# Sixteen modulation units moved into the first attention, and 26 ticks of the second group dealt over the first selection

## The reference

```python
mod = silu(c) @ w_mod + b_mod                    # 6 x 1024 per stream
sh1, sc1, gt1, sh2, sc2, gt2 = split(mod, 6)
h = rmsnorm(x, norm1_gain) * (1 + sc1) + sh1
gq, gk, gv, gr, glr, dq, dk, dv, gates = split(h @ w_in)
y_a = gla(gq, gk, gv, decay(glr)) * silu(gr) @ w_gla_out      # gated linear attention, 4 heads
y_b = diff_attend(rope(norm(dq)), rope(norm(dk)), dv) @ w_diff_out   # two softmax maps a head, 8 heads
x = x + gt1 * ((sigmoid(g_a) * y_a + sigmoid(g_b) * y_b) @ w_out)
h2 = rmsnorm(x, norm2_gain) * (1 + sc2) + sh2
q = h2 @ w_pq                                    # 8 retrieval heads, two halves of 128
v1, i1 = top_k(q1 @ sub_keys1.T, 16); v2, i2 = top_k(q2 @ sub_keys2.T, 16)
sc, ci = top_k(v1[:, None] + v2[None, :], 16)    # 16 of 256 pairs: experts idx, weights g
x = x + gt2 * sum_k(g * gelu(h2 . peer_u[idx]) * peer_v[idx])
```

## Time and profile before

| | |
|---|---|
| time, median of 3 runs | 4507.81 us (4505.8 to 4512.99) |
| profiled execution | 4508.04 us, of it the span of the trace 4505.9 |
| TensorE, VectorE, ScalarE, GpSimd busy | 69, 60, 31, 27% of the span |
| bytes moved | 1531.57 MB, of them the gathers 1107.36 |
| first gather issued / first dots / last dots' products | 494.1 / 509.5 / 4491.5 us |

### The profile page before, as it was taken

How to read it: one execution, slowest core, us unless ns; L and a number is a source line. 1 busy time by engine, 2 the same in 40 slices (tenths; PEclk the granted TensorE clock), 3 DMA queues, 4 the chain that set the end, 5 groups by cost and what they waited for, 6 DMA issues and landing times.

```text
span 4505.9 us, 48754 instructions
## 1 busy us (share of the span) xinstructions
PE 3110.6 (69%) x15864; PEld 1988.0 (44%) x15864; DVE 2683.7 (60%) x7531; ACT 1402.5 (31%) x2980; POOL 1234.7 (27%) x1067
## 2 busy tenths in 40 slices
PE   5776498797878769668786688757776776433333
PEld 3666376485555337446453366534333454200000
DVE  1132634623866884536868864466679845686675
ACT  2341346602255550112555621033446401000000
POOL 0000111101223332322233322322334323344443
PEclk7778699898878789879788799878778788655555
DMA  7546565678989999999899999999999999999997
GB/s 268 187 150 240 195 244 207 229 261 308 373 320 385 360 365 381 386 367 383 323 406 360 345 391 368 391 353 365 359 381 402 405 388 404 401 399 410 400 408 329
DMA packets 285716, 1531.57 MB, mean 340 GB/s; under 512 B 48136, under 2 KB 93288, under 8 KB 112760
## 3 DMA queue, kind: packets, MB, share of 16 engines
q0 software_dynamic: 152064, 1107.36, 62.1%
q1 hardware_dynamic: 133400, 421.09, 25.5%
HBM read 1487.21 MB, written 40.01 MB: 339 GB/s over the span
## 4 chain that ended last, share of the span: by engine, by line
DMA 22%; PE 21%; DVE 13%; issue 6%; ACT 3%; SPq 2%; POOL 1%; DVEq 0%; ACTq 0%; POOLq 0%
DMA rt_ring<-in_peer_uv,rt_few_idx 13%; PE rt_acc L853 5%; DVE rt_ring L1618 5%; PE pair L610 4%; PE pair L599 3%; DMA dense<-scratch_mod 3%; DMA scratch_scores<-dense 3%; PE bank L610 2%; PE pair L766 2%; PE bank L599 2%; DVE rt_diag L1629 1%; DMA w<-in_weights 1%; DVE negmax L1465 1%; DMA scratch_vh<-dense 1%; POOL rt_ring L1671 1%
## 5 line engine op out<-in xcount | busy, mean ns | idle before, releaser
L1671 POOL DMA_INDIRECT rt_ring<-in_peer_uv,rt_few_idx x1056 | 1231.3, 1166 | 3238.2 <-PE rt_acc L853 2566.3
L1618 DVE SCALAR_TENSOR_TENSOR rt_ring<-rt_ring,rt_h 128x1024 f32<-128x1024 f32 x1056 | 1261.8, 1221 | 400.8 <-DMA rt_ring<-in_peer_uv,rt_few_idx 370.3
L853 PE MATMUL rt_acc<-rt_ring,rt_diag 128*32 128x512 f32 x4224 | 770.1, 804 | 656.8 <-DVE rt_diag L1629 655.9
L610 PE MATMUL pair<-dense,w 128*128 128x256 f32 (+2 forms) x3024 | 585.4, 352 | 23.5 <-DMA w<-in_weights 22.7
L599 PE MATMUL pair<-w,dense 128*128 128x256 f32 (+1 forms) x2304 | 556.5, 401 | 32.3 <-DMA w<-in_weights 26.9
L610 PEld LDWEIGHTS pair<-dense,w 128*128 128x128 f32 x3024 | 505.3, 195 | 138.8 <-issue 65.6
L853 PEld LDWEIGHTS rt_acc<-rt_ring,rt_diag 128*32 128x32 f32 x4224 | 100.7, 122 | 999.2 <-DVE rt_diag L1629 869.0
L1180 ACT ACTIVATE rt_act_dot<-rt_dot 128x2 f32<-128x2 f32 x528 | 106.7, 203 | 1365.5 <-DVE rt_ring L1618 1353.7
L599 PEld LDWEIGHTS pair<-w,dense 128*128 128x128 f32 (+1 forms) x2304 | 435.8, 192 | 181.1 <-issue 64.6
L1629 DVE TENSOR_SCALAR rt_diag<-cst,rt_act_dot,rt_few_prob 128x32 f32<-128x32 f32 x1056 | 266.4, 297 | 155.9 <-ACT rt_act_dot L1180 144.7
L610 PE MATMUL bank<-dense,w 128*128 128x256 f32 (+2 forms) x1456 | 287.3, 355 | 5.3 <-DMA w<-in_weights 4.1
(11 more groups left out here) (233 smaller groups left out, 3172.4 us busy)
## 6 DMA issues: line engine op xcount, KB each, us to landing
w<-in_weights SPq DMA_DIRECT2D x284, 1024.0 KB
rt_ring<-in_peer_uv,rt_few_idx POOLq DMA_INDIRECT x1056
rt_h<-scratch_h SPq DMA_DIRECT2D x132, 128.0 KB
dense<-scratch_mod SPq DMA_DIRECT2D x22, 512.0 KB, 17.9
dense<-in_x_prompt SPq DMA_DIRECT2D x16, 512.0 KB, 7.2
scratch_scores<-dense SPq DMA_DIRECT2D x64, 128.0 KB
rt_sc<-scratch_scores SPq DMA_DIRECT2D x8, 1024.0 KB
rt_x<-scratch_x SPq DMA_DIRECT2D x132, 32.0 KB
```

Of the source, the lines that this page charges most:

```text
L610: mm = nc.tensor.matmul(bank[b][:, 0:n], wt[:, k * CH + j * P:k * CH + (j + 1) * P], src[:, k, 0:n], start=(k == 0), stop=(k == KC - 1))
L853: mm = nc.tensor.matmul(acc[u % 2][a * T:(a + 1) * T, :], diag[b % 2][:, i, :], slot[:, D + c * BANK:D + (c + 1) * BANK], start=(q == 0), ...
L1618: dt = nc.vector.scalar_tensor_tensor(up, up, 1.0, h2[u % 2][:], ALU.mult, ALU.mult, accum_out=dot[:, b % 2, i:i + 1])
L1671: nc.gpsimd.indirect_dma_start(ring[n % RING][:], None, d["peer_uv"], bass.IndirectOffsetOnAxis(ap=few_idx[u % 2][:, c:c + 1], axis=0)).th ...
```

## The change

The late modulation's 16 units leave the dk and dv blocks. They stand one behind each of the 16 attention ticks of tile 0, in the order of the loads too. They sum in `rt_acc`, the banks of the routed part, which is idle then; their rows lie in the last buffers of `rt_ring`, as do bias and gain of all six parts. Tile 0's attention no longer takes k and v through the weight ring, but as two transfers at the first dq tick into a third ring buffer. The bank rotation of dk and dv of tile 0 goes over six banks, not five. In `sequence()` the first 26 ticks of group 1 (4 norm, 14 dk, 8 dv) move from the steps into the selection of tile 0: eight before its first step, 18 spread over the steps behind. The rest of group 1's ticks is dealt over the same 38 steps.

```diff
-ARENA, FILLS = 12928, 7
+EARLY, EARLY_1 = 26, 8
+ARENA, FILLS = 12928, 8
...
-    late = [("mod", part, u) for part in range(2, 6) for u in range(4)] if g == 0 else []
     for kind in ("dk", "dv"):
-        for i in range(4):
-            names += [(kind, i)] + late[:2]
-            late = late[2:]
+        names += [(kind, i) for i in range(4)]
...
-    names += [("kv", m) for m in range(len(kv_loads(g)) + kv_lag(g))]
+    if g == 0:
+        names += [("mod", part, u) for part in range(2, 6) for u in range(4)]
+    else:
+        names += [("kv", m) for m in range(len(kv_loads(g)) + kv_lag(g))]
...
-            late(i if kind == "dk" else 4 + i)
...
-    out.extend((("at", g, k), c) for k, c in enumerate(attend_costs(g)))
+    late = [("mod", 2 + u // 4, u % 4) for u in range(16)] if g == 0 else []
+    for k, c in enumerate(attend_costs(g)):
+        out.append((("at", g, k), c))
+        if late:
+            if late[0][2] == 0 and late[0][1] > 2:
+                out.append((("modrow", late[0][1] - 1), 0.5))
+            out.append((late.pop(0), 1.0))
+    assert not late
+    if g == 0:
+        out.append((("modrow", 5), 0.5))
...
-    fill = [tick for tick, _ in ticks(0)] + select(GROUPS[0][0]) + [("unit", 0), ("unit", 1)]
...
+    chain, early, pos = select(GROUPS[0][0]), EARLY, 0
+    fill = [tick for tick, _ in ticks(0)] + chain[:1]
+    for i, step in enumerate(chain[1:]):
+        upto = EARLY_1 + (early - EARLY_1) * i // (SELECT - 6)
+        fill += [tick for tick, _ in lane[pos:min(early, upto)]] + [step]
+        pos = min(early, upto)
+    fill += [("unit", 0), ("unit", 1)]
+    spent = sum(c for _, c in lane[:pos])
...
-    nxt, steps, spent, pos = 2, [], 0.0, 0
+    marks[0], nxt, steps = spent, 2, []
...
+        mbias = ring[RING - 1][:, 0:6 * CH].rearrange("p (m c) -> p m c", c=CH)
+        mrow = ring[RING - 1][:, 6 * CH:8 * CH].rearrange("p (m c) -> p m c", c=CH)
+        mgain = ring[RING - 2][:, 0:2 * CH].rearrange("p (m c) -> p m c", c=CH)
+        k_first = ring[RING - 3][:, 0:D].rearrange("p (h t) -> p h t", h=DH)
+        v_first = ring[RING - 3][:, D:2 * D].rearrange("p (h c) -> p h c", h=DH)
...
+                late = part_ > 1
+                if late:
+                    dst, n = acc[part_ % 2], part_ - 2
+                    if u == 0 and part_ > 3:
+                        pe.wait_ge(late_free, part_ - 3)
...
-                    slot = (g, "kv", kv_load_of(g, x))
-                    wt = weights(slot)
+                    if g == 0:
+                        pe.wait_ge(kv_first, 32)
+                        keys_of = k_first[:, h, :]
...
-                    elif g == 0:
-                        act.wait_ge(md_row, 6)
-                        for i in range(2):
-                            act.wait_ge(md_out[i], 128)
...
+                    if g == 0 and tick == 0:
+                        stored(0)
+                        sp.dma_start(k_first, d["kT"][:, :, 0:P].rearrange("h p t -> p h t")).then_inc(kv_first, 16)
+                        sp.dma_start(v_first, d["vh"][:, :, 0:VD].rearrange("h p c -> p h c")).then_inc(kv_first, 16)
```

More of the change, by code:

```diff
@@ L149, in add @@
         out.extend(((kind, g, i), cost) for i in range(count))
[L151 to L156, removed]
     if g == 0:
@@ L457, in trunk @@
         acc = [ctx.enter_context(nc.psum_tensor(f"rt_acc{u}", [P, BANK], F32)) for u in range(2)]
-        ALL, FIVE = list(range(6)), list(range(5))
+        ALL = list(range(6))
         const_in, filled, act_step, dve_step = sem("const_in"), sem("filled"), sem("act_step"), sem("dve_step")
@@ L554, in mod @@
                 wt = weights((0, "mod", part_, u))
-                if u == 0:
-                    b, n = take(("mod", part_), [5] if part_ > 1 else ALL)
+                late = part_ > 1
[3 more added lines that the diff above has]
+                        pe.wait_ge(late_free, part_ - 3)
+                elif u == 0:
+                    b, n = take(("mod", part_), ALL)
                     pe.wait_ge(bank_free[b], n)
                     pe.wait_ge(c_ready, 1)
-                b, n = sessions["mod", part_]
+                if not late:
+                    b, n = sessions["mod", part_]
+                    dst = bank[b]
                 for kk in range(2):
                     for q in range(4):
-                        mm = nc.tensor.matmul(bank[b][q * 32:(q + 1) * 32, 0:CH], c_pad[:, 2 * u + kk, :],
+                        mm = nc.tensor.matmul(dst[q * 32:(q + 1) * 32, 0:CH], c_pad[:, 2 * u + kk, :],
                                               wt[:, (kk * 4 + q) * CH:(kk * 4 + q + 1) * CH],
                                               start=(u == 0 and kk == 0), stop=(u == 3 and kk == 1))
-                if u == 3:
+                if u == 3 and late:
+                    mm.then_inc(late_made, 1)
+                    released[0, "mod", part_, u] = (late_made, n + 1)
+                elif u == 3:
                     mm.then_inc(bank_made[b], 1)
@@ L616, in rotary @@
                 nt = len(GROUPS[g])
-                among = FIVE if g == 0 and kind == "dk" else ALL
+                among = ALL
                 if kind == "dk" and n == 0:
@@ L641, in dv @@
                     i, ti = n // nt, n % nt
-                    released[g, "dv", i] = tokens(("dv", g, i, ti), weights((g, "dv", i)), ti, hT, FIVE if g == 0 else ALL)
+                    released[g, "dv", i] = tokens(("dv", g, i, ti), weights((g, "dv", i)), ti, hT, ALL)
             def gla_qk(kind, g, p, j):
@@ L752, in attend @@
                     n, nk = width(t), key_count(t)
-                    slot = (g, "kv", kv_load_of(g, x))
-                    wt = weights(slot)
+                    if g == 0:
+                        pe.wait_ge(kv_first, 32)
+                        keys_of = k_first[:, h, :]
+                    else:
+                        slot = (g, "kv", kv_load_of(g, x))
+                        keys_of = weights(slot)
                     wide = nk > BANK or (x > 0 and key_count(GROUPS[g][units[x - 1][1]]) > BANK)
@@ L775, in attend @@
                     n, tiles = width(t), key_tiles(t)
-                    slot = (g, "kv", kv_load_of(g, x) + kv_lag(g))
-                    v = weights(slot)[:, D:].rearrange("p (t c) -> p t c", c=VD)
+                    if g == 0:
+                        v = v_first[:, h:h + 1, :]
+                    else:
+                        slot = (g, "kv", kv_load_of(g, x) + kv_lag(g))
+                        v = weights(slot)[:, D:].rearrange("p (t c) -> p t c", c=VD)
                     pe.wait_ge(at_copied, session_of[G] + 1)
@@ L890, in finished @@
             if kind == "at":
-                return [(a[0], "kv", m) for m in kv_done[a[0]].get(a[1], ())]
+                return [(a[0], "kv", m) for m in kv_done[a[0]].get(a[1], ())] if a[0] > 0 else []
             if kind == "merge":
@@ L1227, in modrow @@
                 i = part_ % 2
-                b, before = sessions["mod", part_]
                 if part_ == 0:
@@ L1661, in _ @@
         def _(pool):
-            for dst, value in ((c_pad[:], 0.0), (arena[:, 4608:6656], 0.0), (state[:], 0.0), (rms[:], 1.0), (ams[:], 1.0),
+            for dst, value in ((c_pad[:], 0.0), (mbias, 0.0), (mgain, 0.0), (state[:], 0.0), (rms[:], 1.0), (ams[:], 1.0),
                                (eps[:], EPS), (one[:], 1.0)):
```

22 lines of the change are left out of this document (15 added, 7 removed).

## The result

The changed kernel takes **4442.9 us** (median of 4 runs, 4440.85 to 4450.89) against 4508.0 (4 runs): ratio 0.9858, 95% interval 0.9845 to 0.9871, so about 64 us (1.4%) faster. The forecast was 4424, in a range from 4405 to 4445. The profiled execution is 63.7 us shorter than the one before (span 4442.2 against 4505.9).

A forecast was written before the change was run, and what follows sets the result against it. No engine is full; up to the first selection's end one tile's work runs alone with a different limit per stretch, then TensorE limits, and DMA from 1104. Sum: 4508.0 - 47 + 8 - 45 = 4424 us, range 4405 to 4445.

The forecast's parts named there:

- Part 1: Tile 0's dk and dv without late modulation: 47 us in place of 94.3, a gain of 47, bounds 35 to 57.
- Part 2: Late modulation's units enter tile 0's attention, mostly hidden after the first seven ticks: +8 us, bounds +1 to +31.
- Rival A: Attention pays in full, each tick waiting for its load: +31 in place of +8, 4447 us; chance 0.12.
- Part 3: 26 ticks dealt over the selection: product 53 us earlier less 8 for steps, a gain of 45, bounds 15 to 58.
- The first selection step: On VectorE, 23.4 us later behind the first eight ticks; the selection's end 36 us later.
- The step that failed: Behind the selection, the next product waits through ScalarE for the first dots: 550 instead of 603.4, 53 us earlier.
- Steps pushed into the rest: Five steps formerly done before the product spread over the later gla and attention chains: 5 to 15 us, taken as 8.
- The remainder: From the last keys of group 1 to the end, both programs alike: 3402 us, within 10.
- B: Early ticks give nothing, the later first gather taking back the steps' gain: 4469 us; chance 0.13.
- C: More than forecast: dk and dv 37 us, attention +3, Part 3 at 58: 4396 us; chance 0.08.
- D: Slower: the first gather, late by 72 us through VectorE's waits, sets the end: 4541 us; chance 0.04.
- E: No change: the first gather sets the end, with the expected delay of 36 us: 4505 us; chance 0.03.

The follow-up runs named there:

- experiment 7: Changed kernel with the 16 late units placed in attention ticks 6 to 15, none in 0 to 5: 4454.1 us, ratio 0.9879.
- experiment 3: Kernel before with only the 26 ticks dealt over the selection, late modulation left in dk and dv: 4486.0 us, ratio 0.9945.
- experiment 2: Changed kernel with no ticks dealt over the selection, only the late modulation moved: 4471.5 us, ratio 0.9913.
- Experiment 4: Changed kernel with 28 early ticks instead of 26, and 4 instead of 8 ahead of the selection: 4424.5 us, ratio 0.9809.
- Experiment 1: Changed kernel with 28 instead of 26 ticks dealt over the selection, so the last value stores precede the first units: 4427.0 us, ratio 0.9819.
- the sixth: On top of experiment 5, the second group's keys due 22 instead of 26 steps ahead of its first unit: 4431.1 us, ratio 0.9832.
- experiment 5: On top of Experiment 4, 12 more second-group ticks behind the first two units' requests, ahead of the first dots: 4429.5 us, ratio 0.9818.
- experiment 8: Changed kernel with the second routed unit's 16 small requests moved from the selection's end to the sixth step: 4430.5 us, ratio 0.9831.
- experiment 9: Experiment 4 with the second routed unit's 16 small requests moved to the sixth step: 4409.2 us, ratio 0.9792.
- experiment 10: Experiment 5 with the second routed unit's 16 small requests moved to the sixth step: 4403.0 us, ratio 0.9776.

## Why the prediction was right, and where it was off

**What bounds the kernel.** Right: no work was removed, all gains are waits, and what was won by the keys' end mostly arrived (63.7 us of 70.4).

**Part 1, -47.** It gave 51.9. dk and dv took 42.4 us. The k stores again stood in the way, but for 3.9 us, not 7:

```profile
59.53 6.49 SPq L1794 DMA_DIRECT2D out_k_prompt<-dense  x2
64.71 0.43 DVE L1353 TENSOR_TENSOR dense<-dense 128x256 f32<-128x256 f32 x1 [3.86 <-DMA out_k_prompt<-dense]
```

dv then started at 69.8, 26.4 us after dk and not 29, and its four blocks ran in 15.9 us. I had taken 18, in the middle between the low-clock block of the earlier trace rows and the fast ones of the earlier trace rows; the row below has 64 products in 16.08 us, 4.0 a block:

```profile
69.84 16.08 PE L623 MATMUL pair<-w,dense 128*128 128x256 f32 x64
```

**Part 2, +8.** It was +6.5, for the reason given. From the first score to the transpose in the eighth tick it took 12.3 us before and 18.1 now (I had said 19 to 24), which is 5.9 of the 6.5; from there on ScalarE's chain hides the units. TensorE:

```profile
204.26 0.80 PE L794 MATMUL pair<-rt_ring,dense 64*128 64x128 f32 x4 [0.76 <-ACT dense L1010]
205.00 1.93 PE L583 MATMUL rt_acc<-w,c_pad 128*32 128x256 f32 x16
...
212.05 1.07 PE L583 MATMUL rt_acc<-w,c_pad 128*32 128x256 f32 x16
...
221.38 1.07 PE L583 MATMUL rt_acc<-w,c_pad 128*32 128x256 f32 x16 [1.31 <-DMA w<-in_weights]
222.39 0.33 PE L769 MATMUL bank<-cst,dense 128*128 128x128 f32 x1
...
231.52 1.93 PE L583 MATMUL rt_acc<-w,c_pad 128*32 128x256 f32 x16
```

Rival A fails: the units' products waited for their loads 2.8 us in all, their weight loads into TensorE 4.0. The mean granted clock of the stretch went from 0.50 to 0.79 with TensorE busy 34.7 of 47.8 us where it had been 17.5 of 41.3, and inside it nine units took 1.07 us each, six 1.93 or 1.94, and one 1.25. The Trainium skill (TensorE: Matmul & The Clock Gate, section on the HAM clock gate) states the direction, that activity lifts the throttled clock; the trace agrees, with 0.79 against 0.50. The measured +6.5 lies halfway between the +5 that I had named for a level that rises and my +8. It didn't rise for good: the three units from 231.52 to 239.09 take 1.93 or 1.94 again, the first of them behind gaps of 2.4 and 0.5 us. The price of a wrong place is known from experiment 7: +20 in place of +6.5.

**Part 3, -45: this term was mis-sized; it gave 23** (70.4 at the keys' end, less the 47.2 by which the last keys of tile 0 came earlier, at 375.9 instead of 423.1). Alone, in experiment 3, it gives 19.4 by trace and 16 to 33 by time; on top of experiment 2 it is 27.3 by trace. Step by step:

- The first selection step was to come 23.4 us later relative to the keys of tile 0: 22.4. The selection's end 36: 33.4. Both right. Experiment 4 shows 6 us of this to be VectorE's wait at the head.
- The step that failed: "The next product needs ScalarE, which waits for the first dots: 550." With the parts 1 and 2 as measured, that is 503, and 522.0 is 19 us behind it. ScalarE didn't wait for the first dots, which began at 496.1, but until 519.0 for the last store of values, and the product came at 522.0. I had counted the ticks up to the 26th and taken the place behind them for free, though two dv ticks were left out of the dealing. They hold no product, only one eviction on ScalarE (at 466.16, 0.38 us) and the last four stores on SyncE. For tile 0 I had written that ScalarE waits at gq for the last v store; for the second group I didn't ask where that store now stands in SyncE's list. Experiment 1 puts them in front: 500.9, within 2 us of the forecast.
- Steps pushed into the rest, +8: 11.1 (500.6 to 511.7 us from the product to the keys' end). TensorE has 32 more products there, four steps of eight, and is busy 13.4 us longer. I had counted five steps; the fifth's products, at 604.47, stand inside the stretch in both kernels. Four steps at 1.06 us are 4.2; the rest goes with the lower granted clock, 0.88 against 0.91, in the two rows shown above (busy time multiplied by clock is 396 and 397). What lowers the clock there is open.

**The remainder.** The claim was that from 1104 on both programs take the same 3402 us, within 10. It is 3408.5, 6.6 more, so the claim held within its margin. I suspected the banks, whose rotation the change shifts; experiment 3 keeps it and has 3413.7. Over the traces of this study (but the sixth's, whose keys are due later) the same stretch takes 3396.5 to 3420.2 us: 3401.1, 3409.0, 3413.7, 3420.2 and 3403.3 in experiments 1 to 5, then 3403.5, 3397.8, 3398.5 and 3396.5 in experiments 7 to 10. No part of the change goes with the long ones: the two longest, 3413.7 and 3420.2, come from executions that were 14.5 and 14.6 us above the median of their kernels. The three shortest are those of experiments 8 to 10, which share the second unit's later requests and also the chip; which of the two it is, or chance, is open. With runs of one kernel up to 32 us apart (experiment 3), a difference of 7 is no effect that these traces can show.

**The rivals.** B, that the early ticks give nothing, falls by experiment 3. C is half right in its first term (dk and dv at 42.4, halfway from 47 to its 37), and in no other. D and E needed the delayed gather to set the end; it was delayed by 33 us as feared, and the stretch shrank by more. The forecast stood 19 us too low by the median, 20 by the profiled execution (4444.0): parts 1 and 2 were 8 better than said (47 against 39), part 3 22 worse, the remainder 7 worse. That the time stayed in the range, by 2 us, is in part luck: without the 8 us more of parts 1 and 2 the same error in part 3 would have put it near 4451.

## What to carry to other kernels

When work is moved ahead of a burst of transfers, move it to its last store: a tick that only stores is cheap in every engine's busy time and can still hold a buffer, and behind the burst it cost 21 us here. When the first wait behind a stage is removed, look at once at who is next in SyncE's list; here the order of its requests came with 10 and 28 us at the keys' end (experiments 9 and 10), ScalarE's order without it with a loss of 8 (experiment 5). And a plan that cuts a list by count should cut it where a buffer is released.

## What the runs showed of the hardware

- A store of 128 KB landed 4.9 us after its issue in front of ten gathers of 1 MB (experiment 1), and 22.6 and 24.8 us after it behind them (changed kernel, experiment 8), with the view's DMA share at 1.03 and 1.02; in experiment 1 it was 0.76 meanwhile.
- Sixteen small requests of one unit hold SyncE for 9 to 10 us (476.4 to 486.1 in the changed kernel's trace), with four groups of four that start 2.8, 2.6, 2.4 and 2.0 us apart, the 4 KB ones first and no shorter than those of 128 and 32 KB. I hadn't counted that as a price for what is queued behind.
- A late unit takes 1.93 us at 205.0, at the head of the attention, and 1.07 at 212.05, with TensorE without a gap in between; at 231.52, behind a gap of 2.4 us and one of 0.5, it takes 1.93 again. The mean granted clock of the stretch is 0.79, before it was 0.50.
